# First pair of experts: tokens picked by a one-hot product on TensorE instead of an indirect gather, and gate selections around the rank sums

## The reference, cut to what matters

```
scores = sigmoid(x @ router_w);  sel = scores + router_bias
g_best = argmax over groups of the sum of the group's top 2 of sel
idx    = top 2 of sel inside g_best;  wsel = scores[idx] / sum(scores[idx])
a, up  = x @ w_gate[e], x @ w_up[e]
y      = sum over the two experts of (silu(a) * up * gate) @ w_down[e]
x      = x + g2 * y
```

## Time and profile before

| what | value |
|---|---|
| median of 3 runs | 958.73 us (957.72 to 960.43) |
| profiled execution, its own time | 962.28 us |
| its span, first to last instruction | 960.4 us |
| TensorE busy | 806.8 us (84%) |
| VectorE busy | 378.3 us (39%) |
| ScalarE busy | 270.5 us (28%) |
| GpSimd busy | 95.1 us (10%) |
| DMA moved | 232.21 MB, mean 242 GB/s |
| mean granted TensorE clock | 0.913 of full |

### The profile page before, as it was taken

One profiled execution on the slowest core, in us unless ns is written; L12 is line 12 of the kernel. 1 busy time (PEld: TensorE's weight loads), 2 busy tenths in 40 slices (PEclk: granted clock), 3 DMA queues, 4 the chain that ended last, 5 costly groups with the idle time before them and its releaser, 6 DMA issues.

```text
span 960.4 us, 11464 instructions
## 1 busy us (share of the span) xinstructions
PE 806.8 (84%) x4035; PEld 443.6 (46%) x4035; DVE 378.3 (39%) x844; ACT 270.5 (28%) x631; POOL 95.1 (10%) x146
## 2 busy tenths in 40 slices
PE   4779999999879988999760878879899989997760
PEld 0237665535434465555330445546544565553230
DVE  3375673354353341422114255475532414221114
ACT  1242112200540242222113235645521422221111
POOL 3200000001000013000004011220200120000002
PEclk9889999999989997999995879999999969999875
DMA  9991174379960297999988854202135679999955
GB/s 293 363 326 45 44 172 152 109 239 319 302 246 0 88 331 277 401 412 412 412 341 267 306 181 175 90 22 69 46 129 222 241 275 377 413 411 411 353 205 197
DMA packets 85055, 232.21 MB, mean 242 GB/s; under 512 B 7188, under 2 KB 17101, under 8 KB 84681
## 3 DMA queue, kind: packets, MB, share of 16 engines
q1 hardware_dynamic: 72706, 193.89, 55.5%
q0 software_dynamic: 8576, 27.38, 8.7%
q10 hardware_dynamic: 3720, 10.25, 2.9%
HBM read 216.60 MB, written 17.78 MB: 244 GB/s over the span
## 4 chain that ended last, share of the span: by engine, by line
PE 59%; DMA 16%; DVE 8%; issue 7%; SPq 3%; ACT 3%; DVEq 1%; POOLq 1%; POOL 0%; ACTq 0%
PE ps L868 53%; DMA ring<-in_moe_w_up_dram 5%; PE ps L875 4%; SPq L654 2%; DMA ring<-in_w_mod_dram 2%; DMA ring<-in_moe_w_down_dram 2%; DMA arena<-in_moe_w_up_dram 2%; PE ps L1095 2%; DVEq L1841 1%; SPq L637 1%; DVE negmax L1894 1%; DMA arena<-y_rows,rows_out 1%; DMA hT<-h_rows,rows_in 1%; DMA h_rows<-xn 1%; DVE xn L2285 1%
## 5 line engine op out<-in xcount | busy, mean ns | idle before, releaser
L868 PE MATMUL ps<-arena 128*64 128x256 f32 (+13 forms) x1084 | 233.8, 460 | 30.2 <-DMA arena<-in_moe_w_down_dram 7.5
L868 PEld LDWEIGHTS ps<-arena 128*64 128x64 f32 (+4 forms) x1084 | 125.5, 174 | 120.6 <-issue 71.8
L868 PE MATMUL ps<-ring,arena 128*64 128x256 f32 (+1 forms) x864 | 128.5, 441 | 14.8 <-DMA ring<-in_moe_w_up_dram 7.6
L868 PE MATMUL ps<-ring,hT 128*128 128x512 f32 (+2 forms) x384 | 133.8, 508 | 6.5 <-issue 5.9
L868 PEld LDWEIGHTS ps<-ring,hT 128*128 128x128 f32 x384 | 73.2, 192 | 65.0 <-issue 60.6
L868 PEld LDWEIGHTS ps<-ring,arena 128*64 128x64 f32 x864 | 61.0, 138 | 65.6 <-issue 40.0
L875 PE MATMUL ps<-ident,arena 128*128 128x128 f32 (+2 forms) x332 | 51.0, 293 | 19.7 <-DVE hT L1900 4.6
L1513 ACT ACTIVATE arena<-ps 128x256 f32<-128x256 f32 (+5 forms) x88 | 38.6, 454 | 94.4 <-PE ps L868 87.8
L2225 DVE TENSOR_TENSOR arena<-arena,ps 128x128 f32<-128x128 f32 x37 | 10.7, 288 | 134.8 <-ACT arena L1618 134.8
L868 PE MATMUL ps<-hT,ring 128*128 128x384 f32 x192 | 62.1, 486 | 0.0
L868 PE MATMUL ps<-ring,condT 128*32 128x512 f32 x384 | 52.6, 675 | 7.1 <-DMA ring<-in_w_mod_dram 6.5
(11 more groups left out here) (295 smaller groups left out, 841.5 us busy)
## 6 DMA issues: line engine op xcount, KB each, us to landing
ring<-in_w_mod_dram SPq DMA_DIRECT2D x48, 1024.0 KB, 9.0
ring<-in_moe_w_down_dram SPq DMA_DIRECT2D x24, 1024.0 KB, 17.7
ring<-in_moe_w_gate_dram SPq DMA_DIRECT2D x42, 512.0 KB, 14.2
ring<-in_moe_w_up_dram SPq DMA_DIRECT2D x42, 512.0 KB, 16.2
arena<-in_moe_w_gate_dram SPq DMA_DIRECT2D x32, 512.0 KB, 8.7
arena<-in_moe_w_up_dram SPq DMA_DIRECT2D x32, 512.0 KB, 10.1
arena<-in_moe_w_down_dram SPq DMA_DIRECT2D x13, 1024.0 KB, 12.1
ring<-in_ev_w_in_dram SPq DMA_DIRECT2D x9, 1024.0 KB, 13.1
```

The costliest lines, as they stand in the source:

```text
L868: mm = pe.matmul(out, lhsT, rhs, **kw)
```

## The change

The first pair's tokens no longer come by a gather. VectorE builds from `hit` and the pair table a matrix `first_hit` (tokens by slots, with a 1 where a token sits in a slot of pair 0), and TensorE multiplies the transposed token tiles with it: 24 products of 128x128 stationary and 128 moving columns, accumulated over the three token tiles, land in the same banks as the transposes did. The pair table must be kept, so the token numbers go to another place (`id_table`). Gathers 1 to 7 are left. Since `htok` is now read by `first_pair`, gathers 3 to 6, which overwrite it or come behind, wait until its second half is done. Both gate selections move up by one place: `mod_select` 0 before the rank sums, `mod_select` 1 between these and the index products.

```diff
         B.stage(f"mod{l}.{G2}.1", 1, (6,))
+        B.stage(f"modsel{l}.{G2}.0", 2, (0, 1))
         B.stage(f"rank{l}", 1, (2,))
-        B.stage(f"modsel{l}.{G2}.0", 2, (0, 1))
+        B.stage(f"modsel{l}.{G2}.1", 2, (4, 5))
         B.stage(f"idx{l}", 1, (3,))
-        B.stage(f"modsel{l}.{G2}.1", 2, (4, 5))
...
-                for c in range(NPAIR):
-                    if c >= 2 * NT:
-                        pool.wait_ge(xt_full[1][l], c - 2 * NT + 1)
+                for c in range(1, NPAIR):
+                    if c >= NT:
+                        pool.wait_ge(xt_full[1][l], max(c - 2 * NT, 0) + 1)
...
+                def first_pair():
+                    pe.wait_ge(first_ready, l + 1)
+                    for half in range(2):
+                        for q in range(4):
+                            k = 4 * half + q
+                            for t in range(NT):
+                                mm = product(ps[XT_BANKS[half]][:, q * P:(q + 1) * P], htok[:, t, k * P:(k + 1) * P], first_hit[:, t, :], carries=False,
+                                             start=t == 0, stop=t == NT - 1)
+                        mm.then_inc(xt_full[half][l], 1)
...
-                main_turn(0)
+                first_pair()
...
                 mod_product(f"ffn{l}", 1)
+                mod_select(f"ffn{l}", 0)
...
                 fill_inc(mm, f"rank{l}")
-                mod_select(f"ffn{l}", 0)
+                mod_select(f"ffn{l}", 1)
                 bank = claim(f"idx{l}")
...
                 fill_inc(mm, f"idx{l}")
-                mod_select(f"ffn{l}", 1)
...
-                dve.tensor_tensor(tabs, tabs, ids..., ALU.mult)
-                dve.drain().then_inc(hit_ready[l], 1)
+                dve.tensor_tensor(id_table..., tabs, ids..., ALU.mult)
+                dve.drain().then_inc(hit_ready, 1)
+                for t in range(NT):
+                    dve.tensor_scalar(first_hit[:, t, :], hit[:, t, :], tabs[:, 0, t, 0:1], None, ALU.mult)
+                settle()
+                for t in range(NT):
+                    dve.scalar_tensor_tensor(out=first_hit[:, t, :], in0=hit[:, NT + t, :], scalar=tabs[:, 1, t, 0:1], in1=first_hit[:, t, :], op0=ALU.mult, op1=ALU.add)
+                dve.drain().then_inc(first_ready, 1)
```

More of the change, by code:

```diff
@@ L435, in build_step @@
         hit_over = view(7232, 2 * NT, HALF)
+        first_hit = view(7232, NT, P)
+        id_table = plan[:, 1280:1328]
         mixed = view(2816, 2, 512)
@@ L549, in build_step @@
         per_layer = lambda name: [sem(f"{name}{l}") for l in range(2)]
-        plan_sums, plan_ready, hit_ready, rows_ready = per_layer("plan_sums"), per_layer("plan_ready"), per_layer("hit_ready"), per_layer("rows_ready")
+        plan_sums, plan_ready, hit_ready, rows_ready = sem("plan_sums"), sem("plan_ready"), sem("hit_ready"), sem("rows_ready")
+        first_ready = sem("first_ready")
         over_hit, over_idx, over_rows = per_layer("over_hit"), per_layer("over_idx"), per_layer("over_rows")
@@ L572, in blocks_of @@
         def blocks_of(eng, l):
-            eng.wait_ge(plan_ready[l], 1)
+            eng.wait_ge(plan_ready, l + 1)
             return eng.value_load(meta[0:1, l, 0:1], min_val=1, max_val=NOVER)
@@ L788, in _ @@
                 pool.drain()
-                pool.wait_ge(rows_ready[l], 1)
-                for c in range(NPAIR):
-                    if c >= 2 * NT:
-                        pool.wait_ge(xt_full[1][l], c - 2 * NT + 1)
+                pool.wait_ge(rows_ready, l + 1)
+                for c in range(1, NPAIR):
+                    if c >= NT:
+                        pool.wait_ge(xt_full[1][l], max(c - 2 * NT, 0) + 1)
                     pool.indirect_dma_start(xg[c], None, h_rows[l], bass.IndirectOffsetOnAxis(ap=rows_in[:, c:c + 1], axis=0)).then_inc(
@@ L1227, in moe @@
                 mod_product(f"ffn{l}", 1)
+                mod_select(f"ffn{l}", 0)
                 bank = claim(f"rank{l}")
                 pe.wait_ge(in_route, 48 * (l + 1))
-                pe.wait_ge(plan_sums[l], 1)
+                pe.wait_ge(plan_sums, l + 1)
                 product(bank[:, 0:48], before, both, start=True, stop=False)
@@ L1237, in moe @@
                 fill_inc(mm, f"rank{l}")
-                mod_select(f"ffn{l}", 0)
+                mod_select(f"ffn{l}", 1)
                 bank = claim(f"idx{l}")
-                pe.wait_ge(hit_ready[l], 1)
+                pe.wait_ge(hit_ready, l + 1)
                 for i in range(2 * NT):
-                    mm = product(bank[:, 0:NPAIR], hit[:, i, :], pair_ids[:, 8 * i:8 * i + 8], start=i == 0, stop=i == 2 * NT - 1)
+                    mm = product(bank[:, 0:NPAIR], hit[:, i, :], id_table[:, 8 * i:8 * i + 8], start=i == 0, stop=i == 2 * NT - 1)
                 fill_inc(mm, f"idx{l}")
-                mod_select(f"ffn{l}", 1)
                 experts(l)
@@ L2099, in route @@
                 settle()
-                dve.tensor_tensor(both, masks[:, 0:48], masks[:, 48:96], ALU.add).then_inc(plan_sums[l], 1)
+                dve.tensor_tensor(both, masks[:, 0:48], masks[:, 48:96], ALU.add).then_inc(plan_sums, 1)
             def plan_rows(l):
@@ L2123, in plan_rows @@
                 settle()
-                dve.tensor_tensor(tabs, tabs, ids[:, :].unsqueeze(1).unsqueeze(3).broadcast_to([P, 2, NT, NPAIR]), ALU.mult)
-                dve.drain().then_inc(hit_ready[l], 1)
+                dve.tensor_tensor(id_table.rearrange("p (m t c) -> p m t c", m=2, t=NT), tabs, ids[:, :].unsqueeze(1).unsqueeze(3).broadcast_to([P, 2, NT, NPAIR]), ALU.mult)
+                dve.drain().then_inc(hit_ready, 1)
[5 more added lines that the diff above has]
+                dve.drain().then_inc(first_ready, 1)
                 bank = filled_wait(dve, f"idx{l}")
                 drain_inc(dve.tensor_copy(rows_in[:, :], bank[:, 0:NPAIR]), f"idx{l}")
-                dve.drain().then_inc(rows_ready[l], 1)
+                dve.drain().then_inc(rows_ready, 1)
             ranks, size = plan[:, 1080:1128], plan[:, 1128:1144]
@@ L2181, in plan_blocks @@
                 dve.tensor_copy(meta[0:1, l, 0:1], count[0:1, :])
-                dve.tensor_copy(meta[0:1, l, 1:2 + NOVER], owners[0:1, :]).then_inc(plan_ready[l], 1)
+                dve.tensor_copy(meta[0:1, l, 1:2 + NOVER], owners[0:1, :]).then_inc(plan_ready, 1)
                 dve.tensor_tensor(ranks, ranks, past, ALU.add)
```

## The result

The changed kernel's median is 962.99 us (19 runs, 954.22 to 968.80), that of the kernel before 958.73 us (19 runs, 953.41 to 962.88). The ratio is 1.0047, 95% interval 1.0025 to 1.0069: slower by about 4.5 us, forecast 962.5. The executions of one kernel spread over 10 us and more, more than the first three runs of before let one expect, and this matters for reading the profiles: the profiled execution of the changed kernel has a span of 957.3 us, shorter than the 960.4 of before, although the kernel is slower. The two places have to be read apart.

A forecast was written before the change was run, and what follows sets the result against it. The weight stream was taken to set the experts' end; later gathers left in it cost 1.5 us in layer 0 and 2.4 in layer 1, so 958.7 + 3.9 gave 962.5 us, range 955.0 to 966.0.

The forecast's parts named there:

- stream of weights: Main experts: weight loading and the gathers left in it set their end; 2.7 to 5.9 us slower, chance 0.50.
- the price I took: Weight stream: each gather still unfinished at the first refill costs the stream 1.5 us.
- that rival: Experts' end: TensorE sets it and late gathers are absorbed; 2.7 us faster, 956.0 us, chance 0.17.
- The sizes in layer 0: First gate product 370.4 us, first refill 372.3, 4.9 gathers left, stream free of gathers 1.5 us later.
- The products: Before the first expert: 24 one-hot products take 7.6 us, 0.45 each at half clock and 0.24 at full.
- The six operations: VectorE's added work beside the index products: 2.0 us, at most 2.2, hidden there.
- the full-clock branch: Index products at full clock: the cast queues behind VectorE's added work, and TensorE's start of the experts loses 0.7 us.
- Layer 1: First gate product 785.7 us, first refill 787.6, 4.9 gathers left, stream free of gathers 2.4 us later.
- selection 0: Gate selection before the rank sums: fills a 2.47 us gap free in layer 0, costs 0.3 us in layer 1.
- "by the rows" reading: Head: clock stays half into the 24 products, rising 4.0 us after their start, despite the filled gap.
- the first rival: Head: clock stays full, products take 5.8 us and start 0.7 earlier; 1.1 us faster, 957.6 us, chance 0.18.
- The sum: Both layers together: 1.5 us and 2.4 us later, 3.9 us slower in all.

The follow-up runs named there:

- e8: The changed kernel with each of the 24 products done twice into the same sum; ratio to the kernel before 1.0295.
- e6: The changed kernel once more, unchanged, for a second profile; ratio to the kernel before 1.0038.
- e7: The changed kernel with gather 3 sent to the tile that gather 0 left free, so gathers 1 to 3 leave without a wait; ratio to the kernel before 1.0013.
- e4: The changed kernel with other buffers for the gathers, so gathers 1 to 5 leave without a wait; median 956.89 us, ratio to the kernel before 0.9987.
- e2: The changed kernel with both gate selections back at their old places, the one-hot product kept; ratio to the kernel before 1.0111.
- e5: The kernel before once more, unchanged, for a second profile; ratio 0.9991.
- second pair: The second profiles of the kernel before (e5) and the changed kernel (e6), both unchanged; ratios 0.9991 and 1.0038.
- e10: The kernel of e4 with both feed-forward gate selections left out, products and copies; ratio to the kernel before 0.9974, not to be compared.
- e9: The kernel of e4 run again unchanged; median 956.32 us, ratio to the kernel before 1.0000.

## Why the prediction held, step by step

**The bound was the stream of weights.** Shown. Over 24 stretches (two layers, twelve profiles) M - R follows the MB of gathers left at the refill: 96.4 us plus 2.8 us for each MB, correlation 0.94, scatter 0.6 us. That is 1.5 us for a gather, the price I took; the slope is uncertain by 0.2, so plain bytes at 413 GB/s (2.4 us for a MB) are not excluded. What TensorE did before the refill does not enter: e8 delayed the refill by 5 to 6 us, M followed in full and M - R stayed. That alone speaks against slack in TensorE and not for the stream, since a TensorE that set the end would be late by as much. What puts that rival out is e6, e7 and e4: one head (R - E 18.4), and M - R 103.2, 102.1 and 99.0 by the gathers alone. The Trainium skill, page "DMA: Bandwidth & Descriptors", section "Queues, rings and completion order", says that each DMA engine takes turns between the queue rows that have work; the fitted price agrees with gathers and weights sharing engines so that each byte of the one delays the other.

**The sizes in layer 0.** First gate product 370.27 (said 370.4), first refill 372.25 (372.3), 4.6 gathers left (4.9), last main expert 1.6 us later (1.5). This execution had the same full clock at the second modulation product as the one the rows were read from, and most have not; so close a fit is in part luck.

**The products.** 8.27 and 7.20 us, in e6 7.22 twice (said 7.6, ends 7.0 and 8.6). At full clock 0.233 each in e2 (0.24).

**VectorE.** The six operations take 1.6 us (0.68 and 0.88), where I took 2.0 and bounded by 2.2. Where the clock stayed high through the index products they are not quite hidden: TensorE is idle 0.5 to 0.8 us before the 24 products, by size what the full-clock branch said (0.7). The releaser in three of the four stretches is the end of these operations themselves (L2145) and not, as I had it, the cast behind them.

**Layer 1 was mis-sized in its first pair.** I said first gate product 785.7 and 2.4 us lost. It came at 784.46, 1.2 us earlier, mostly because I had the index products at half clock (2.6 us) when they took 1.48; and nothing was lost in those two profiles, also because the first profile of before had an M - R of 101.9 there, where e5 has 99.9. By the second pair the loss is 2.3 us: the sum is near mine, though not by my steps.

**The wrong step.** For selection 0 I wrote "so it fills that gap and costs nothing" of layer 0, and "I charge 0.3 us" of layer 1. The 2.47 us gap of the earlier trace rows is there only where the second modulation product runs at full clock. In such an execution selection 0 did cost nothing (rank sums at 354.44 against 354.47), but these are four of the twelve layer-0 stretches and none of layer 1; in e5 the gap is 0.82. There selection 0 delays the rank sums by 0.95 us in both layers, and VectorE's next step with them by 0.8 and 0.5 (from E: 2.4 to 3.2 and 2.7 to 3.2). Against that stands the clock. From rank sums to refill the changed head takes 16.6 us, the old one 18.1 to 18.3 (e5), and e10's, with the low clock, 19.3 and 19.6: without the clock the one-hot head would not be shorter than the old one. My "by the rows" reading, that the clock would be low from before the 24 products on, was the other half of the error. In three of the four changed stretches it fell only after their start, and e10 shows that the selections are why. The Trainium skill, page "TensorE: Matmul & The Clock Gate", Part 1, says that activity releases the throttle and that idleness brings it back. e10 agrees with it: TensorE is idle for 2.98 us before the index products, which then run at 0.50. But the clock fell in the changed kernel too, with TensorE idle for no more than 1.2 us at a time from selection 0 on, and was 0.50 through much of the 24 products. So the first rival did not come about.

**The sum.** By the second pair 2.6 and 2.3 us, 4.8 in all; by both pairs 3.2; timed 4.3 us between the medians; predicted 3.9. Its parts by the second pair, a layer: 0.95 for selection 0, minus 1.6 for the head, plus 3.1 for gathers that used to fly in the stream's pause. The last is the mechanism that was forecast, and e4, e7 and e9 show it. That the total came so near is in part luck: the cost of selection 0 that I left out and the clock that I had too low are errors of opposite sign.

## What to carry to other kernels

Where a stream of weights bounds a phase, look for its pauses and count what flies in them: here a gather that flew in the pause was free, and the same gather, issued 4 to 5 us later, cost its 1.5 us. Work that reads a buffer for longer holds up whatever is to overwrite it; here a gather was saved and four others were pushed out of the pause, and giving the first of them other buffers won 6 us back. Read marks inside the phase, not the span, when executions of one kernel differ by 1%, and look at the clock just before the mark that you count from: here it moved the mark by 1.6 us.

## What the runs showed of the hardware

Taking work out of TensorE's gaps made the path longer: without the two selections (4.0 us of products at full clock in each layer) the granted clock was 0.50 at the index products, and the first refill left 1.8 and 2.4 us later behind VectorE's masks than with them. A gap on TensorE can itself hang on the clock: the gap before the rank sums was 2.47 us where the product ahead of it ran at full clock (1.9 us) and 0.8 us where it did not (3.4 us). And the overflow blocks, whose program is the same in all these kernels, took between 41.9 and 48.5 us in layer 1 from one profile to another; what makes the difference I did not find.
